# Output weights loaded row by row and begun in the stage before, and ScalarE and VectorE reordered within a prompt step, in a two-layer hybrid decoder step

## What is computed

```python
h = rms_norm(x, norm_g[i])
z = h @ w_in                        # branch inputs | gate | memory query | memory gate
# layer 1, per head and query block (12 heads; prompt keys, or 2048 paged past keys + 4 new)
z = q @ k.T * HEAD_DIM ** -0.5 + bias
log_beta = log_sigmoid(z)
log_rem = where(mask, log_beta - z, 0)
later = cumsum(log_rem, reverse) - log_rem
a = where(mask, exp(log_beta + later), 0);  branch = a @ v
y = concat([branch * silu(gate), mo * silu(mgate)]) @ w_out[i]      # w_out: (2048, 1024)
x = x + y
```

## Time and profile before

| | us |
|---|---|
| median of three runs (2681.95 to 2691.65) | 2687.8 |
| the profiled execution, whole | 2685.18 |
| its span, first to last instruction | 2683.4 |
| TensorE busy (90% of the span) | 2418.1 |
| VectorE busy (37%) | 988.4 |
| ScalarE busy (32%) | 861.4 |

### The profile page before, as it was taken

The page is one execution under the profiler, slowest core; times in us unless marked ns, Lnnn a source line. Parts: engine busy times, 40 slices in busy tenths (PEclk is TensorE's granted clock), DMA queues, the critical chain, the costliest instruction groups (busy, mean ns, idle before and its releaser), DMA issues. The chain is left out here.

```text
span 2683.4 us, 42572 instructions
## 1 busy us (share of the span) xinstructions
PE 2418.1 (90%) x17253; PEld 2002.8 (75%) x17253; DVE 988.4 (37%) x1469; ACT 861.4 (32%) x1662; POOL 185.6 (7%) x377
## 2 busy tenths in 40 slices
PE   4699999998599699999999999779999999995999
PEld 4699999896488589999999998655555555542787
DVE  5421334105311321111112111467777777753211
ACT  4321111114210222112110011356666666674100
POOL 0000000102000000000001120211211111110000
PEclk8899999999799789999999998879999999998999
DMA  5422201302633232233231122658999999973432
GB/s 173 136 81 82 82 18 34 112 2 102 231 99 95 100 113 81 98 128 130 94 121 58 45 88 79 191 173 319 362 370 385 369 384 365 364 252 132 141 96 71
DMA packets 203708, 426.34 MB, mean 159 GB/s; under 512 B 22965, under 2 KB 116257, under 8 KB 203497
## 3 DMA queue, kind: packets, MB, share of 16 engines
q1 hardware_dynamic: 193209, 387.58, 41.3%
q0 software_dynamic: 10304, 36.05, 3.6%
HBM read 361.75 MB, written 62.37 MB: 158 GB/s over the span
## 5 line engine op out<-in xcount | busy, mean ns | idle before, releaser
L80 PE MATMUL o_bank<-o_w_hi,o_y_hi 128*128 128x512 f32 x576 | 228.9, 397 | 60.4 <-DVE o_w_lo L1254 59.5
L81 PE MATMUL o_bank<-o_w_lo,o_y_hi 128*128 128x512 f32 x576 | 227.4, 395 | 0.0
L82 PE MATMUL o_bank<-o_w_hi,o_y_lo 128*128 128x512 f32 x576 | 227.0, 394 | 0.0
L80 PEld LDWEIGHTS o_bank<-o_w_hi,o_y_hi 128*128 128x128 f32 x576 | 110.0, 191 | 88.8 <-issue 46.7
L1902 DVE STREAM_TRANSPOSE b_kt<-bf_kraw 128x768 f32<-128x768 f32 x172 | 166.2, 967 | 0.0
L1378 ACT ACTIVATE i_stage<-i_bank 128x352 f32<-128x352 f32 x108 | 50.1, 465 | 347.9 <-PE i_bank L82 347.9
L2065 PEld LDWEIGHTS b_krow<-b_kt,b_qd 128*32 128x32 f32 x3072 | 105.3, 111 | 70.0 <-issue 54.8
L80 PE MATMUL i_bank<-h_hT_hi,h_w_hi 128*128 128x352 f32 x432 | 140.7, 326 | 2.1 <-PEq L75 2.1
L2012 PE MATMUL b_zbank<-bf_qh,bf_kh 128*128 128x512 f32 (+3 forms) x288 | 134.2, 549 | 8.5 <-PEq L75 8.5
L80 PE MATMUL i_bank<-h_hT_hi,i_w_hi 128*128 128x352 f32 x432 | 141.1, 327 | 0.0
L2065 PE MATMUL b_krow<-b_kt,b_qd 128*32 128x128 f32 x3072 | 140.9, 280 | 0.0
(11 more groups left out here) (308 smaller groups left out, 5567.0 us busy)
## 6 DMA issues: line engine op xcount, KB each, us to landing
bf_vpage<-in_cache_sb_v_dram SPq DMA_DIRECT2D x128, 768.0 KB, 7.2
bf_kraw<-in_cache_sb_k_dram SPq DMA_DIRECT2D x172, 384.0 KB
l_w<-in_cache_sb_k_dram SPq DMA_DIRECT2D x84, 384.0 KB
o_y<-scratch_yT SPq DMA_DIRECT2D x18, 1024.0 KB, 6.6
o_w<-in_w_out_dram SPq DMA_DIRECT2D x16, 1024.0 KB
l_w<-in_w_in_sb_dram SPq DMA_DIRECT2D x8, 1536.0 KB
i_w<-in_w_in_sb_dram SPq DMA_DIRECT2D x8, 1536.0 KB
l_w<-in_cache_mem_k_dram SPq DMA_DIRECT2D x16, 512.0 KB, 4.3
```

Source lines behind the costliest of these rows:

```text
L80: pe.matmul(out, stat_hi, mov_hi, start=first, stop=False)
L81: pe.matmul(out, stat_hi, mov_lo, start=False, stop=False)
L82: return pe.matmul(out, stat_lo, mov_hi, start=False, stop=last)
```

## The change

1. The output weights are loaded in 16 transfers of one block (512 KB) through five raw buffers. Two of the 16 blocks are loaded and split, three more are loaded raw, and most of tile 0's `y` (layer 0: blocks 0 to 11, layer 1: all but blocks 10 and 11) is loaded and split in the stage before. In layer 0 that is memory attention: the loads stand where `following.fetch` is, the splits at the ends of prompt tiles 2 to 6. In layer 1 it is the stick stage: the loads stand on SP at step 130 of 144, the splits behind steps 133 to 137 (ScalarE) and 134 to 138 (VectorE).
2. In the output stage the rest of `y` is loaded first; its split stands before block 5, that of tile 1's `y` before block 13. The residual `x` of tile 0 is loaded last.
3. The buffers of both stages share one arena. `vh`, `gh`, `kn`, `qn` and `vn` no longer fit before the stick stage, and their loads move to its start, as SP's first instructions.
4. In a prompt step ScalarE now does `log_part(t+1)`, the exponential of t, `high(t+1)`, `evacuate(t+2)`; VectorE does `exponent(t)` ahead of `softplus(t+1)`.
5. One more group of semaphores is cleared, with a barrier, at the end of each layer.

```diff
+KM = 2 * D // P
+RAW, SPLIT = 5, 2
+class OutAhead:
+        self.order = list(range(KM)) if i == 0 else list(range(10)) + [12, 13, 14, 15, 10, 11]
+        self.early, self.late = [([(0, 4), (4, 8), (8, 12)], (12, 16)), ([(0, 5), (5, 10), (12, 16)], (10, 12))][i]
+    def fetch(self, sp):
+        for at in range(SPLIT):
+            self.weights(sp, at)
+        for r in self.early:
+            self.rows(sp, r, self.yl)
+        for at in range(SPLIT, RAW):
+            self.weights(sp, at)
+    def high(self, act, t):
+        n = t - 2
+        if 0 <= n < SPLIT:
+            act.wait_ge(self.wl[n], 16)
+            act.activation(self.w_hi[n][:, :], self.w[n], ACT.Copy).then_inc(self.whi, 1)
+        if SPLIT <= n < SPLIT + len(self.early):
+            act.wait_ge(self.yl, 16 * len(self.early))
+            a, b = self.early[n - SPLIT]
+            act.activation(self.y_hi[:, a:b, :], self.y[:, a:b, :], ACT.Copy).then_inc(self.yhi, 1)
...
 def out_phase(nc, c, A, yT, i, source, target, begun):
             def _(sp):
+                begun.rows(sp, begun.late, s["yl"])
+                for at in range(RAW, KM):
+                    sp.wait_ge(begun.wlo, at - RAW + 1)
+                    begun.weights(sp, at)
+                    if at == 2 * RAW:
+                        load_y(1)
+                load_x(0)
...
+                for at in range(SPLIT, KM):
+                    if at == RAW:
+                        part(0)
+                    if at == KM - 3:
+                        part(1)
+                    act.wait_ge(wl[at % RAW], 16 * (at // RAW + 1))
+                    act.activation(w_hi[at][:, :], w[at % RAW], ACT.Copy).then_inc(begun.whi, 1)
...
 def stick_phase(nc, c, A, O, S, begun):
             def _(sp):
+                begun.fetch_rest(sp)
                 sp.dma_start(gs[:, :, :], S["gT"][:, :, SEQ:T].rearrange("h p t -> p h t")).then_inc(s["gsl"], 16)
...
+                    if e == ("P", NSTEP - 14):
+                        sp.wait_ge(s["ktr"], PG * NU)
+                        for n in range(2):
+                            sp.wait_ge(ys[n], 16 * 5)
+                        out.fetch(sp)
...
                 def step(t):
-                    if t + 2 < NSTEP:
-                        evacuate(t + 2)
                     if t + 1 < NSTEP:
                         log_part(t + 1)
-                    if t + 1 < NSTEP:
-                        high(t + 1)
                     n = steps[t][4]
                     act.wait_ge(s["tsub"], t + 1)
                     act.activation(a[:, t % 3, 0:n], a[:, t % 3, 0:n], ACT.Exp).then_inc(s["ax"], 1)
+                    if t + 1 < NSTEP:
+                        high(t + 1)
+                    if t + 2 < NSTEP:
+                        evacuate(t + 2)
...
+                    exponent(t)
                     if t + 1 < NSTEP:
                         softplus(t + 1)
-                    exponent(t)
```

More of the change, by code:

```diff
@@ L1057, in _ @@
                     gated(t)
+                    following.low(dve, t)
                 dve.wait_ge(s["sel"], 1)
@@ L1194, in out_phase @@
         x = k.sb("x", [P, 2, D])
         bank = k.ps("bank", 4)
-        wl = [k.sem(f"wl{n}") for n in range(2)]
         xl = [k.sem(f"xl{n}") for n in range(2)]
         ol = [k.sem(f"ol{n}") for n in range(2)]
-        s = {n: k.sem(n) for n in "yl whi wlo yhi ylo ready added".split()}
+        s = {n: k.sem(n) for n in "yl yhi ylo ready added".split()}
         N = TILES + 1
-        NW = KM // CH
         tok = lambda t: t * P if t < TILES else LAST
+        part_of = lambda t: slice(0, KM) if t else slice(*begun.late)
@@ L1525, in fetch, with fetch_rest @@
         self.keys(sp, 0)
+        for u in range(1, NK):
+            self.keys(sp, u)
+        for n in range(NV - 2):
+            self.values(sp, n)
+    def fetch_rest(self, sp):
+        O, S = self.O, self.S
         sp.dma_start(self.vh[:, 0, :, :], O["sbv_p"][0, 0, :, 0, :].rearrange("(t p) d -> p t d", p=P)
@@ L1531, in fetch, with high, low @@
         sp.dma_start(self.vn[:, :], O["sbv_s"][0].rearrange("b t h d -> (b t) (h d)")).then_inc(self.added, 16)
-        for u in range(1, NK):
-            self.keys(sp, u)
-        for n in range(NV - 2):
-            self.values(sp, n)
-class NothingAhead:
-    def allocate(self):
+    def high(self, act, t):
         pass
-    def fetch(self, sp):
+    def low(self, dve, t):
         pass
@@ L1614, in stick_phase @@
         a = k.sb("a", [P, 3, 512])
-        kt = [k.sb(f"kt{n}", [P, HH, HD // Q, P]) for n in range(2)]
         qd = k.sb("qd", [P, 2, HEADS * QP])
@@ L1825, in _ @@
                         step(e[1])
+                    if e[0] == "P" and e[1] >= NSTEP - 13:
+                        act.wait_ge(s["kr"], NU)
+                        out.high(act, e[1] - NSTEP + 13)
                     if e == ("N", 0):
@@ L1997, in _ @@
                         sample_output(e[1])
+                    if e[0] == "P" and e[1] >= NSTEP - 12:
+                        dve.wait_ge(s["kr"], NU)
+                        out.low(dve, e[1] - NSTEP + 12)
                     if e == ("P", NSTEP - 1):
```

154 lines of the change are left out of this document (103 added, 51 removed).

## The result

The changed kernel takes 2620.86 us, median of four runs (2618.68 to 2625.36), against 2684.88 for the kernel before (four runs, the three named above among them); the ratio is 0.9759 with a 95% interval of 0.9736 to 0.9781. The forecast was 2621. Between the two medians lie 64.0 us, where 66.7 were forecast. Its profiled execution takes 2618.68 us, its span 2617.0, against 2685.18 and 2683.4.

A forecast was written before the change was run, and what follows sets the result against it. TensorE was taken to bound the stick stage's middle, DMA close behind; output tile 0 waited for weights. 43.2 + 26 - 1 - 2.5 + 6 - 3.5 - 1.5 = 66.7 us off 2685.2: 2618.5, about 2621 median; range 2600 to 2648.

The forecast's parts named there:

- Output tile 0, 43.2: Both output stages: TensorE starts with the stage and tile 0 takes 27.5 us, saving 21.4 and 21.8, together 43.2 us.
- ScalarE waits until about 19: Output tile 0: tile 1's y lands late, ScalarE waits until about 19 us, block 13's low part comes at about 24.5.
- Rival (b): Output tile 0 is feed-bound at 34 us, 13 us less gained, 2634 us in all; chance 0.13.
- Order, 26: Stick stage: the new order within a step returns 26 us of TensorE's idle time; bounds 0 and 43.
- 5 of 13.0, since the clock (0.90) and first loads set part of it: Start of the stick stage: the new order returns 5 of TensorE's 13.0 us idle; clock and first loads limit it.
- Its idle time the most that can come back: Stick stage: TensorE's own work is the floor, so the order can return at most its idle time, 43.4 us.
- Splits put into the stick tail, 1: Tail of the stick stage: the added splits cost 1 us, 4 if the cover were gone.
- Layer 0's memory attention, 2.5 (bounds 0 and 6): Layer 0's memory attention: splits fall into ScalarE's gaps of about 0.75 us, two blocks overrun; cost 2.5 us.
- Moved loads, +6 and -3.5: Five moved loads: 6 us gained in layer 1's memory attention (bounds 2, 8), 3.5 lost at the stick stage's start.
- Barriers, 1.5: Ends of the layers: the two added barriers cost 1.5 us, bounds 0.5 and 3.
- Rival (a), DMA caps the middle: Middle of the stick stage: DMA is the limit, it keeps its 440 us, 2635 us in all; chance 0.15.
- Rival (d), VectorE held at `exponent(t)`: Stick stage: VectorE stands at `exponent(t)`, `softplus(t+1)` and transpositions queue behind; slower, 2713 us at a 5.3 us step; chance 0.03.

The follow-up runs named there:

- run 6: The changed kernel with the load of tile 1's x taken from behind tile 1's y and put behind tile 0's x: 2620.82 us.
- run 7: The changed kernel with tile 1's y loaded in four 256 KB pieces behind weight blocks 10 to 13 and split behind the last block: 2616.13 us.
- run 8: The changed kernel with a pad of 32 bytes on the right side of SBUF: 2615.31 us.
- run 9: The changed kernel with a 32-byte pad and the arena places of y and the two early weight blocks exchanged: 2616.25 us.
- run 10: The kernel before the change, with only the even tiles' y_hi and y_lo moved to the right side of SBUF: 2690.11 us.
- run 11: The changed kernel with a pad of 96 bytes, putting the whole right side of SBUF at multiples of 128 bytes: 2606.97 us.
- run 2: The kernel before the change with the new order of both ScalarE and VectorE and nothing else: 2651.13 us.
- run 5: The changed kernel with only half of each later value page loaded, all instructions and waits kept: 2619.13 us, one run.
- run 12: The changed kernel with a 96-byte pad on SBUF's right side and tile 1's y loaded in four pieces: 2601.39 us.

## Why the prediction was right, and where its terms were not

- **Result.** 2621.0 forecast, 2620.86 measured. "Faster" held. The mechanisms were in the main the forecast's, but the exactness is luck: the stick stage gave 11.9 us more, the output stages 12.2 less; layer 1's memory attention gave 2.65 more, which the 2.6 of chance ahead of the change took back. The drop between medians is 64.0 and not 66.7; the difference is that the kernel before came out at 2684.9 with a fourth run, where the forecast had started from 2687.8.
- **Output tile 0, 43.2.** Measured 36.8 from tile 0. "With the stage" was right. The step that failed is "ScalarE waits until about 19": it waits for block 11 and not for `y`, since the prediction has no hold of the queue behind `y(1)` in it. The load of `y(1)` holds the next issue for 4.1 to 4.5 us, block 11 is late before block 13 can be, and TensorE idles 2.94 there. Runs 6 and 7 show it; with pieces tile 0 lasts 26.6 and 27.6, so 27.5 was a fair figure for what the product and feeding ask. Rival (b), feed-bound at 34, didn't come: over tile 0 the loads ran at 274 and 276 GB/s, against 236 and 234 before. By the 2 us of fixed cost of the Trainium skill (DMA: Bandwidth & Descriptors, Anatomy of one DMA — SWDGE (gpsimd) path), which the page gives for transfers that GpSimd issues, an estimate is 35 us for the eleven blocks in turn; the trace, with several in flight and tile 0 at 30.5 and 29.9, does not agree.
- **The later tiles, not in the sum.** 6.1 us lost. "I take 0.228 at full clock" assumed that a matmul's pace doesn't depend on where its operands are. Runs 8 to 11 show that it does, by 3%, and that no other part of the change has a share.
- **Order, 26.** Measured 36.6, 16.2 of it in the middle for a forecast of 14, 7.0 in the tail for 7, 13.3 at the start for 5. The step that failed is "5 of 13.0, since the clock (0.90) and first loads set part of it": the clock was treated as given, and it rose with the gaps gone. "Its idle time the most that can come back" failed with it: 6.3 of the 9.8 us in the first 12 steps came out of busy time, and 13.5 of the 36.6 in all. By idle time alone the order gave 23.1, where 26 was forecast. The chain itself was right, 3.78 us for the tail's step where 3.9 was said; "ScalarE no longer waits 0.81" was not quite, it waits 0.29.
- **Splits put into the stick tail, 1.** Measured 1.7 in run 2's comparison (149.6 against 147.9). Right.
- **Layer 0's memory attention, 2.5 (bounds 0 and 6).** 3.05 in the pair of profiles, but 6 to 9 us over all traces: mis-sized. "Two blocks overrun it by 0.3 to 0.9" counted only the engine time beyond the gap; behind a piece of `y` TensorE waited too, and the two waits grew by 2.7 and 1.7 us, with a slower pace behind the second.
- **Moved loads, +6 and -3.5.** Measured 8.65, beyond its bound of 8, and 0.4 of wait at the start; the first steps are 1.5 longer than with the order alone. Both were mis-sized, and the kernel gained by it: the last moved load landed in time for all but 0.4 us.
- **Barriers, 1.5.** About 1.2 measured: from the last product of an output stage to its end it is 0.6 us longer in each; right, though no run isolates it.
- **Rival (a), DMA caps the middle.** Refuted: 389 GB/s, and run 5 shows that 304 gives the same steps. The rule of the Trainium skill (DMA: Bandwidth & Descriptors, Where 436 GB/s comes from) that HBM binds at about 358 GB/s would have kept the middle as it was; the trace does not agree.
- **Rival (d), VectorE held at `exponent(t)`.** Not in this kernel: VectorE does wait there now, 28.3 us in the middle, but off the path. Its mirror is real: ScalarE's order alone makes the kernel slower by 0.4%.

## What to carry to other kernels

When two engines hand one chain back and forth, price their orders together: each half of this reorder taken alone gave -18 and +12 us, the two together -36. Give a load of many small rows its own place behind the loads that someone waits for, or cut it, since the queue holds what comes behind it; and look where the allocator puts a matmul's operands, because here one that starts beside a multiple of 128 bytes cost 3% of the product for nothing. A difference between two profiles is worth what several profiles of the same code agree on: one stage of this kernel differs by up to 6 us from one to the next.

## What the runs showed that was not expected

- **Operand alignment.** A float32 matmul of 128x512 with 0.2267 us from start to start takes 0.2333 to 0.2343 when one operand's buffer starts beside a multiple of 128 bytes in the partition (96 matmuls: 21.76 against 22.36 to 22.49 us), and 0.2306 when both do by the same distance. Shown by moving nothing but places.
- **A held queue.** With weights in flight, an issue behind one load of 2048 rows of 512 bytes takes 3.05 to 4.53 us instead of 0.33 to 0.5, whether it loads `x` or weights, in the kernel before too (4.11 and 4.22); as the first loads of an output stage, 1.76 and 1.79. Behind a load of as many bytes in 256 rows of 4 KB it took 0.46 and 0.47. Behind a load of 512 small rows it took at most 0.78 in run 7 and 1.07 in run 12, and 1.6 to 1.9 behind two such loads in a row (the early `y` in layer 0).
- **The clock pays twice.** Taking gaps out of the first 12 steps raised the granted clock there from 0.84 to 0.96 (0.88 to 0.96 over nine traces) and shortened TensorE's busy time by 6.3 us, nearly twice the idle time removed.
- **DMA near a share of one is no bound by itself.** 387 GB/s over 390 us, and 304, give the same time to a tenth of a microsecond.
